# Where the modulation vectors are summed: from TensorE to VectorE, tile by tile

## Chip, cores, metric

One core of one Trainium2 chip. The metric is the device time of one execution in microseconds (us), as the median of several runs. The profile shows one execution, with the time of every instruction and DMA.

## What is computed

A backbone of two layers over 512 latent tokens and 256 context tokens, model width 1024. Every sub-layer (feed-forward half step, mixer, feed-forward half step) is wrapped in an RMSNorm with nine modulation vectors per layer: shift, scale and gate of each of the three sub-layers. There is one set for the latent tokens (from `c`) and one for the context tokens (from `c_ctx`):

```
adaln_in(x, g, m, i)     = rmsnorm(x, g) * (1 + m[3i+1]) + m[3i]
adaln_out(x, y, g, m, i) = x + w * m[3i+2] * rmsnorm(y, g)
m = silu(c) @ w_mod + b_mod          # w_mod of a layer: 1024 x (9 * 1024)
```

All is float32. The context stream ends in the mixer of layer 0 (it is read there and not written), so of the nine context vectors of layer 0 only shift, scale and gate of the first sub-layer and shift and scale of the second are used; of layer 1 none is.

## The kernel before

**Blocks.** The large products are tiled in weight blocks of 128 output columns. A block of 1024 (down stages: 768 or 640) columns per partition comes in over SP's DMA queue into `raw` (a ring of 4 slots), ScalarE makes its high part `w_hi` (`split_hi`, L893), VectorE its low part `w_lo` (`split_lo`, L1297), and TensorE runs three matmuls per 128x128 tile (`three`, L451 to L453). SP loads the next block into a slot when VectorE has split the last one; TensorE waits for `lo_split` before every block. Each engine runs its own program in order.

**Stages.** A feed-forward half step has four stages: gate-up of 24 blocks, down_a of 16 blocks of 768 columns, gate-up of 20, down_b of 16 blocks of 640. `stepped` (L92) runs them in steps of four blocks, mostly as a loop with the first and the last step unrolled. In a gate-up step, for each pair of blocks j, VectorE does two splits ahead, waits for the pair, multiplies (`prod`, L1391), waits for ScalarE's `act_hi` and subtracts (`act_lo`, L1396). In a down step it does two splits ahead, waits for the pair and copies or adds the result to `y` (L1434, L1436). The order of the stages is latent half step (0,0), context half step (0,0) with 256 tokens, the mixer, half steps (0,2), (1,0), the Hyena mixer, half step (1,2). In the context half step's first gate-up VectorE also writes the latent output (`x_out`: L1529, L1530, L1525).

**Modulation.** GpSimd loads `w_mod` in tiles of 128x1024 (512 KB, `load_mods`, L1933) into `mod_raw`, a ring of four; it issues a tile when `mod_used` says that the slot is free. A vector (a "group") is eight tiles. TensorE takes them in `mod_units` (L455): per tile k four matmuls in four column groups, with silu(c) of both streams as weights (32 columns, of which two are used) and the tile as the moving side. The units of a group stand between the blocks of a step, three, three, two and none; in the first step six after the first pair. VectorE copies the sums (`mod_copy`), TensorE turns them (`mod_turn`, L465) and VectorE adds the bias (`mod_finish`). Groups 0 and 1 are done at the start of the kernel, 2 to 7 in the first gate-up (`ffns[0][0]`), 8 in the first context gate-up (two batches of four units), layer 1's first five in the gate-up of 20 blocks of half step (0,2), its last four in down_a of half step (1,0). `gain_pre` and `gain_post` (L1345, L1353) make the scale columns from them.

**GpSimd's queue.** After layer 0's tiles it waits for the mixer, loads `rope`, clears `ak`, and goes on with the mixer's tables; then layer 1's tiles, and what Hyena needs. ScalarE's queue loads the small tables at the start, `rot` and `head_ones` among them.

Of the kernel before, what the change touches and what calls it, by code (L numbers as in the profile page):

```python
# [17 lines left out]
F32 = mybir.dt.float32  # L18
# [5 lines left out]
P = 128  # L24
# [26 lines left out]
SHIFT, SCALE, GATE = range(3)  # L51

# [61 lines left out]

def build(nc, io):
# [10 lines left out]
    for which, half0 in [(0, (0, 2)), (0, None)]:  # L126
        ffns.append([stage("gu", io["gate_up"][which, 0:24], 24, 1024, half0),
                     stage("dn", io["down_a"][which], 16, 768),
# [6 lines left out]
    for which, (half0, half1, down0) in [(1, (None, (1, 0), None)), (2, (None, None, (1, 5)))]:  # L135
# [15 lines left out]
    with ExitStack() as ctx:  # L151
# [7 lines left out]
        with ExitStack() as r:  # L159
# [5 lines left out]
            turns = r.enter_context(nc.sbuf_tensor("turns", [P, 512], F32))  # L165

# [22 lines left out]
        c_silu = sb("c_silu", [P, KT, 32])  # L189
# [11 lines left out]
        rot = sb("rot", [P, P])  # L201
        head_ones = sb("head_ones", [P, P])
# [23 lines left out]
        with region():  # L226
# [6 lines left out]
            mod_row = rb("mod_row", [P, 256])  # L233
            kept_rinv = rb("kept_rinv", [P, SEQ])

        with region():
# [4 lines left out]
            with region():  # L241
                rb("inner", [P, 32 * 256])
                rq = rb("rq", [P, 4, SEQ])
                av = rb("av", [P, ALL // P, P])
            with region():
# [22 lines left out]
        with region():  # L268
# [27 lines left out]
        mod_used, mod_row_ready, mod_turned, mod_ready = map(  # L296
            sem, ("mod_used", "mod_row_ready", "mod_turned", "mod_ready"))
# [8 lines left out]
        rope_landed = sem("rope_landed")  # L306
# [66 lines left out]
        LOADS = 8  # L373
# [68 lines left out]
        def _(pe):  # L442

            at = {"p": 0, "f": 0, "group": 0, "norm": 0, "h": 0}
# [10 lines left out]
            def mod_units(g, ks):  # L455

                for k in ks:
                    pe.wait_ge(mod_landed[k % RING], 16 * (2 * g + k // RING + 1))
                    for j in range(4):
                        ins = pe.matmul(psum[32 * j:32 * j + 32, MODP, 0:256], c_silu[:, k, :],  # L460
# [4 lines left out]
            def mod_turn(g):  # L465
# [3 lines left out]
                ins.then_inc(mod_turned, 1)  # L469

# [36 lines left out]
            def gate_up(s, T, beside=lambda i: None):  # L507
                b0, p0, g0 = s.first, at["p"], at["group"]
# [35 lines left out]
                if s.mods:  # L544
                    at["group"] += s.blocks // 4

            def down(s, T, tiles, beside=lambda i: None):
                b0, p0, g0, f0 = s.first, at["p"], at["group"], at["f"] - tiles
# [1574 lines left out]
```

## Time and profile before

| | us |
|---|---|
| median of 3 runs | 2734.34 (2731.32 to 2734.46) |
| the profiled execution | 2735.59 |
| its span, first to last instruction | 2733.9 |
| TensorE busy | 2504.0 (92%) |
| VectorE busy | 1209.1 (44%) |
| ScalarE busy | 876.5 (32%) |
| GpSimd busy | 111.7 (4%) |
| mean granted TensorE clock | 0.95 |

How to read the profile: a group of instructions is named by its line in the kernel, its engine and operation, and what it writes and reads; then come the count, the busy time and the mean ns of one, and the idle time of the engine before them with what ended it. PE is TensorE, PEld its weight loads, DVE VectorE, ACT ScalarE, POOL GpSimd, SP the sync engine. The chain of waits is followed back from the last instruction to whatever released each step. A float32 matmul that is not of the `three` kind appears as two instructions. Matmul ends are modelled and overlap, so pace is read from starts. Clock 1.00 is 2.4 GHz, 0.50 is 1.2 GHz.

### The profile page before, as it was taken

What the parts mean: (1) busy time and instruction counts of PE and PEld (TensorE: products, weight loads), DVE (VectorE), ACT (ScalarE), POOL (GpSimd) and SP (SyncE); (2) the same over time, 40 slices, a digit from 0 to 9 for tenths busy, and PEclk for the clock granted to TensorE, in tenths of its full rate; (3) what the DMA queues carried; (4) which work ended last, traced back from release to release, by engine and by line L of the source; (5) the groups of instructions that cost most, each with busy time, mean ns of one, the idle gap of its engine ahead of it and who ended that gap; (6) DMA issues with size and microseconds to landing.
All of it is one profiled execution on the core that took longest, in us unless ns stands there. A gap on an engine that the chain in (4) does not pass through costs nothing.

```text
span 2733.9 us, 32899 instructions
## 1 busy us (share of the span) xinstructions
PE 2504.0 (92%) x12514; PEld 1971.3 (72%) x12514; DVE 1209.1 (44%) x1765; ACT 876.5 (32%) x1283; POOL 111.7 (4%) x186
## 2 busy tenths in 40 slices
PE   5899999999899887899999989999989828899997
PEld 2477788899778434778877778778878527788886
DVE  4523233565553676543222353323355385533334
ACT  1422222444431456343222242222244302422222
POOL 1011000000000110000011000100000000000000
PEclk9999999999999899889999989999979969799999
DMA  7566322455312000132356312552212113132322
GB/s 289 196 219 226 128 96 75 151 176 183 130 62 83 31 1 1 62 108 85 100 200 224 130 58 93 193 181 94 91 55 93 70 46 107 49 102 81 108 77 77
DMA packets 91167, 309.53 MB, mean 113 GB/s; under 512 B 10960, under 2 KB 11632, under 8 KB 89776
## 3 DMA queue, kind: packets, MB, share of 16 engines
q1 hardware_dynamic: 67824, 221.75, 24.2%
q0 software_dynamic: 21936, 84.88, 8.7%
q8 instruction: 75, 1.23, 0.2%
q10 hardware_dynamic: 1296, 1.38, 0.1%
q14 instruction: 36, 0.29, 0.0%
HBM read 299.58 MB, written 8.39 MB: 113 GB/s over the span
## 4 chain that ended last, share of the span: by engine, by line
PE 81%; DVE 8%; ACT 4%; DMA 2%; issue 2%; POOLq 0%; POOL 0%; DVEq 0%; ACTq 0%
PE psum L451 24%; PE psum L452 23%; PE psum L453 23%; PE psum L582 2%; DMA mod_raw<-in_w_mod 2%; PE psum L460 2%; PE psum L873 1%; DVE spectrum L359 1%; DVE term L352 1%; PE psum L740 1%; PE psum L604 1%; DVE w_lo L1297 1%; PE psum L862 1%; DVE stats L1767 1%; ACT w_hi L893 0%
## 5 line engine op out<-in xcount | busy, mean ns | idle before, releaser
L451 PE MATMUL psum<-h_hi,w_hi 128*128 128x512 f32 (+1 forms) x2256 | 860.4, 381 | 28.4 <-DVE h_lo L1480 13.7
L452 PE MATMUL psum<-h_lo,w_hi 128*128 128x512 f32 (+1 forms) x2256 | 848.4, 376 | 0.0
L453 PE MATMUL psum<-h_hi,w_lo 128*128 128x512 f32 (+1 forms) x2256 | 847.5, 376 | 0.0
L451 PEld LDWEIGHTS psum<-h_hi,w_hi 128*128 128x128 f32 x2256 | 429.3, 190 | 128.1 <-issue 35.1
L1297 DVE TENSOR_TENSOR w_lo<-raw,w_hi 128x1024 fp32r<-128x1024 f32 (+2 forms) x442 | 470.6, 1100 | 65.3 <-ACT w_hi L893 61.4
L893 ACT ACTIVATE w_hi<-raw 128x1024 fp32r<-128x1024 f32 (+2 forms) x442 | 405.8, 951 | 251.2 <-PE psum L453 243.7
L453 PEld LDWEIGHTS psum<-h_hi,w_lo 128*128 128x128 f32 x2256 | 429.1, 190 | 77.2
L452 PEld LDWEIGHTS psum<-h_lo,w_hi 128*128 128x128 f32 x2256 | 429.8, 191 | 74.0 <-issue 1.0
L451 PE MATMUL psum<-act_hi,w_hi 128*128 128x512 f32 (+1 forms) x880 | 331.5, 377 | 7.5 <-DVE w_lo L1297 5.5
L453 PE MATMUL psum<-act_hi,w_lo 128*128 128x512 f32 (+1 forms) x880 | 329.2, 374 | 0.0
L452 PE MATMUL psum<-act_lo,w_hi 128*128 128x512 f32 (+1 forms) x880 | 329.1, 374 | 0.0
L1391 DVE TENSOR_TENSOR prod<-psum,square 128x512 f32<-128x512 f32 (+1 forms) x110 | 70.2, 638 | 565.5 <-PE psum L453 560.0
L923 ACT ACTIVATE act_hi<-prod 128x512 f32 (+3 forms) x110 | 64.8, 589 | 550.4 <-DVE prod L1391 550.4
L451 PEld LDWEIGHTS psum<-act_hi,w_hi 128*128 128x128 f32 x880 | 166.9, 190 | 44.5 <-issue 13.1
L453 PEld LDWEIGHTS psum<-act_hi,w_lo 128*128 128x128 f32 x880 | 166.8, 190 | 32.0
L452 PEld LDWEIGHTS psum<-act_lo,w_hi 128*128 128x128 f32 x880 | 167.0, 190 | 31.2
L921 ACT ACTIVATE square<-psum 128x512 f32<-128x512 f32 (+1 forms) x110 | 60.7, 552 | 245.2 <-PE psum L453 245.1
L1938 POOL DMA_DIRECT2D mod_raw<-in_w_mod x144 | 76.4, 530 | 1235.0 <-PE psum L460 1095.8
L1434 DVE COPY y<-psum 128x512 f32<-128x512 f32 (+3 forms) x40 | 25.5, 638 | 195.7 <-PE psum L453 195.6
L1396 DVE TENSOR_TENSOR act_lo<-prod,act_hi 128x512 f32 (+3 forms) x110 | 70.3, 639 | 91.7 <-ACT act_hi L923 91.7
L460 PE MATMUL psum<-mod_raw,c_silu 128*32 128x256 f32 x1152 | 82.3, 409 | 27.3 <-DMA mod_raw<-in_w_mod 25.1
L460 PEld LDWEIGHTS psum<-mod_raw,c_silu 128*32 128x32 f32 x1152 | 31.2, 113 | 73.1 <-DMA mod_raw<-in_w_mod 39.6
(229 smaller groups left out, 1812.5 us busy)
## 6 DMA issues: line engine op xcount, KB each, us to landing
raw<-in_gate_up SPq DMA_DIRECT2D x220, 512.0 KB, 4.2
mod_raw<-in_w_mod POOLq DMA_DIRECT2D x144, 512.0 KB, 5.6
raw<-in_down_a SPq DMA_DIRECT2D x80, 384.0 KB, 3.5
raw<-in_down_b SPq DMA_DIRECT2D x80, 320.0 KB, 3.0
raw<-in_hy_in SPq DMA_DIRECT2D x24, 512.0 KB, 3.5
raw<-in_mix_in SPq DMA_DIRECT2D x22, 512.0 KB, 3.5
filt_dram<-made SPq DMA_DIRECT2D x6, 1024.0 KB, 3.8
filt<-filt_dram POOLq DMA_DIRECT2D x2, 3072.0 KB, 10.9
```

Of the source, the lines that this page charges most:

```text
L451: pe.matmul(out, w_hi[:, slot, c:c + P], hi, start=start, stop=False)
L452: pe.matmul(out, w_hi[:, slot, c:c + P], lo, start=False, stop=False)
L453: return pe.matmul(out, w_lo[:, slot, c:c + P], hi, start=False, stop=stop)
L460: ins = pe.matmul(psum[32 * j:32 * j + 32, MODP, 0:256], c_silu[:, k, :], mod_raw[:, k % RING, 256 * j:256 * j + 256], start=(k == 0), sto ...
L582: ins = pe.matmul(psum[:, bank, t:t + 1], src[:, t * P:t * P + P], ones[:, 0:1], start=first and t == 0, stop=last and t == T // P - 1)
L893: act.activation(w_hi[:, slot, 0:cols], raw[:, slot, 0:cols], ACT.Copy).then_inc(hi_split, 1)
L921: act.activation(silu[:, j, 0:T], psum[:, bank, 0:T], ACT.Silu).then_inc(silu_ready, 1)
L923: act.activation(act_hi[:, bass.ds(2 * i + j, 1), 0:T], prod[:, j:j + 1, 0:T], ACT.Copy).then_inc(act_hi_ready, 1)
L1297: ins = dve.tensor_tensor(w_lo[:, slot, 0:cols], raw[:, slot, 0:cols], w_hi[:, slot, 0:cols].bitcast(F32), ALU.subtract)
L1391: ins = dve.tensor_tensor(prod[:, j, 0:T], psum[:, bank, 0:T], silu[:, j, 0:T], ALU.mult)
L1396: dve.tensor_tensor(act_lo[:, fl, 0:T], prod[:, j:j + 1, 0:T], act_hi[:, fl, 0:T].bitcast(F32), ALU.subtract).then_inc(act_ready, 1)
L1938: pool.dma_start(mod_raw[:, k % RING, :], io["w_mod"][layer, v, k]).then_inc(mod_landed[k % RING], 16)
```

## The change

- Groups from 2 on are summed by VectorE. `mod_add` multiplies tile k by its column of silu(c) (one value per partition) and adds it to `mod_acc` (128x1024): `tensor_scalar` for k = 0, `scalar_tensor_tensor` for the rest, each waiting for its tile and for the one before. It stands behind `act_lo` (or behind the copy to `y`), four tiles for each pair of blocks.
- TensorE only adds up over the partitions: `mod_sum`, eight matmuls of a 128x128 piece of `mod_acc` as weights against one column of ones, after the second block of the next step. VectorE adds the bias to the eight columns (`mod_keep`).
- Latent and context streams are now groups of their own. The context gets five vectors: two from groups 0 and 1, as before for both streams, and three (v = 2, 3, 4) in groups 8 to 10. That makes 21 groups instead of 18 (168 tiles instead of 144). Groups 8 to 11 (the fourth is the latent gate of sub-layer 2) are in down_a of the first half step; the context gate-up has none. Layer 1 keeps its places.
- `gain_pre` and `gain_post` wait for fixed counts and make the context's columns only where they are used.
- `mod_acc` needs room: `mod_row` and `kept_rinv` become parts of it, the context's `kept_ctx` is apart, and `rot` and `head_ones` live in the mixer's memory, loaded by GpSimd ahead of `rope` and not by ScalarE at the start. `silu(c)` is made twice, wide for groups 0 and 1 (`c_wide`) and narrow (`c_silu`).

```diff
-    for which, half0 in [(0, (0, 2)), (0, None)]:
+    for which, half0, down0 in [(0, Mods(2, 0, 2, 6), Mods(8, 0, 2, 4, 1, {3: (8, 0)})), (0, None, None)]:
...
-    for which, (half0, half1, down0) in [(1, (None, (1, 0), None)), (2, (None, None, (1, 5)))]:
+    for which, (half0, half1, down0) in [(1, (None, Mods(12, 1, 0, 5), None)), (2, (None, None, Mods(17, 1, 5, 4)))]:
...
+            def mod_sum(g):
+                pe.wait_ge(mod_used, RING + KT * g + KT)
+                for c in range(KT):
+                    ins = pe.matmul(psum[:, MODP, c:c + 1], mod_acc[:, c * P:c * P + P], ones[:, 0:1],
+                                    start=(c == 0), stop=(c == KT - 1))
+                ins.then_inc(mod_summed, 1)
+            def sum_before(s, i):
+                nonlocal pending
+                if not isinstance(i, int) or i:
+                    if s.mods:
+                        mod_sum(s.mods.first + i - 1)
+                elif pending:
+                    mod_sum(pending.first + pending.steps - 1)
+                    pending = None
...
             def gate_up(s, T, beside=lambda i: None):
...
-                        if s.mods:
-                            mod_units(g0, range(6))
+                        sum_before(s, i)
...
+                        if j == 1:
+                            sum_before(s, i)
                         if j == 2:
                             beside(i)
-                        if s.mods:
-                            mod_units(g0 + i, ((0, 1, 2), (3, 4, 5), (6, 7), ())[j])
-                    if s.mods:
-                        mod_turn(g0 + i)
...
             def first_ffns():
...
-                    elif i in (1, 2):
-                        mod_units(g, range(4 * i - 4, 4 * i))
-                    elif i == 4:
-                        mod_turn(g)
...
+            def mod_add(g, who, ks):
+                for k in ks:
+                    dve.wait_ge(mod_landed[k % RING], 16 * (2 * g + k // RING + 1))
+                    src, c = mod_raw[:, k % RING, :], c_silu[:, k, who:who + 1]
+                    if k == 0:
+                        if not isinstance(g, int) or g > 2:
+                            dve.wait_ge(mod_summed, g - 2)
+                        ins = dve.tensor_scalar(mod_acc[:, :], src, c, None, ALU.mult)
+                    else:
+                        dve.wait_ge(mod_used, RING + KT * g + k)
+                        ins = dve.scalar_tensor_tensor(mod_acc[:, :], src, c, mod_acc[:, :], ALU.mult, ALU.add)
+                    ins.then_inc(mod_used, 1)
+            def mod_keep(mods, i):
+                v, who = mods.at(i)
+                dve.wait_ge(mod_summed, mods.first + i - 1)
+                dve.tensor_tensor(mod[:, mods.layer, bass.ds(v, 1), who, :], psum[:, MODP:MODP + 1, 0:KT],
+                                  b_mod[:, mods.layer, bass.ds(v, 1), :], ALU.add).then_inc(mod_ready, 1)
+            def mods_of(s, i, j):
+                if j:
+                    keep_before(s, i)
+                if s.mods:
+                    mod_add(s.mods.first + i, s.mods.at(i)[1], range(4 * j, 4 * j + 4))
...
-                        if s.mods and j == 1:
-                            mod_copy(g0 + i)
...
                         dve.tensor_tensor(act_lo[:, fl, 0:T], prod[:, j:j + 1, 0:T], act_hi[:, fl, 0:T].bitcast(F32),
                                           ALU.subtract).then_inc(act_ready, 1)
+                        mods_of(s, i, j)
                         beside(i, j)
-                    if s.mods:
-                        mod_finish(g0 + i, s.mods[0], s.mods[1] + i)
...
-            load_mods(0)
+            load_mods(0, 0, 0, 8)
+            load_mods(8, 0, 2, 5)
+            load_mod(11, 0, 8)
             pool.wait_ge(block_done, RING + mix_in.first)
+            pool.wait_ge(mod_used, RING + 12 * KT)
+            pool.dma_start(rot[:], io["rot"]).then_inc(rot_landed, 16)
+            pool.dma_start(head_ones[:], io["head_ones"]).then_inc(rot_landed, 16)
             pool.dma_start(rope[:], io["rope"][:, 2:4]).then_inc(rope_landed, 16)
```

`down` is changed like `gate_up` on both engines. `sum_before` and `keep_before` act on the step before; the sum of a stage's last group falls into the next stage.

## Rows read from the trace of the kernel before

**Rows 1.** The page, chain that ended last: shares by engine and by line.

```profile
PE 81%; DVE 8%; ACT 4%; DMA 2%; issue 2%; POOLq 0%; POOL 0%; DVEq 0%; ACTq 0%
PE psum L451 24%; PE psum L452 23%; PE psum L453 23%; PE psum L582 2%; DMA mod_raw<-in_w_mod 2%; PE psum L460 2%; PE psum L873 1%; DVE spectrum L359 1%; DVE term L352 1%; PE psum L740 1%; PE psum L604 1%; DVE w_lo L1297 1%; PE psum L862 1%; DVE stats L1767 1%; ACT w_hi L893 0%
```

**Rows 2.** Windows, PE PEld DVE ACT POOL busy (x), clock, DMA share, GB/s.

```profile
113.67:282.24 168.57, 163.81 (x973) 120.17 (x973) 49.26 (x67) 40.64 (x52) 25.33 (x48) 0.97 0.68 238
...
349.50:458.48 108.98, 108.98 (x482) 90.28 (x481) 35.80 (x39) 29.18 (x38) 0.00 (x0) 1.00 0.27 86
...
1306.30:1373.49 67.19, 67.19 (x289) 54.08 (x288) 20.71 (x25) 15.46 (x18) 0.00 (x0) 1.00 0.32 106
1373.49:1513.19 139.70, 135.05 (x811) 98.81 (x810) 38.41 (x52) 29.16 (x38) 21.11 (x40) 0.99 0.62 217
1729.89:1819.27 89.38, 86.56 (x554) 60.45 (x552) 22.95 (x35) 15.41 (x18) 14.78 (x28) 1.00 0.69 244
```

**Rows 3.** Timeline, PE, first gate-up step: start, us, what, [idle before <- releaser].

```profile
126.15 1.93 PE L460 MATMUL psum<-mod_raw,c_silu 128*32 128x256 f32 x32
131.98 1.08 PE L460 MATMUL psum<-mod_raw,c_silu 128*32 128x256 f32 x8 [3.89 <-DMA mod_raw<-in_w_mod]
...
134.54 0.80 PE L451 MATMUL psum<-h_hi,w_hi 128*128 128x512 f32 x1
...
141.45 0.64 PE L460 MATMUL psum<-mod_raw,c_silu 128*32 128x256 f32 x8
```

**Rows 4.** Timeline, PE, second gate-up step: three units, next block.

```profile
153.85 1.50 PE L460 MATMUL psum<-mod_raw,c_silu 128*32 128x256 f32 x24
155.28 0.50 PE L451 MATMUL psum<-h_hi,w_hi 128*128 128x512 f32 x1
```

**Rows 5.** Windows of three other stretches, columns as in rows 2.

```profile
127.40:141.00 13.60, 9.24 (x55) 5.80 (x44) 3.05 (x3) 2.16 (x3) 3.17 (x6) 0.75 0.87 337
...
75.00:85.00 10.00, 10.00 (x42) 5.84 (x41) 3.92 (x11) 1.78 (x4) 0.00 (x0) 1.00 0.25 105
7.50:31.70 24.20, 9.45 (x62) 2.14 (x66) 10.87 (x21) 5.98 (x12) 3.80 (x7) 1.00 1.02 419
```

**Rows 6.** Timeline, DVE, context gate-up: pairs of splits; units stand in the first.

```profile
540.57 2.36 DVE L1297 TENSOR_TENSOR w_lo<-raw,w_hi 128x1024 fp32r<-128x1024 f32 x2 [1.31 <-ACT w_hi L893]
...
547.75 2.36 DVE L1297 TENSOR_TENSOR w_lo<-raw,w_hi 128x1024 fp32r<-128x1024 f32 x2 [1.05 <-ACT w_hi L893]
...
554.38 2.36 DVE L1297 TENSOR_TENSOR w_lo<-raw,w_hi 128x1024 fp32r<-128x1024 f32 x2 [1.04 <-ACT w_hi L893]
```

**Rows 7.** Timeline, PE: sixteen one-column matmuls and the matmul behind them.

```profile
75.63 0.95 PE L582 MATMUL psum<-ones,sumsq 128*128 128x1 f32 x8
...
77.33 0.68 PE L503 MATMUL psum<-taps,dft_f 128*128 128x512 f32 x1
```

**Rows 8.** Groups of DVE by form: busy us, mean ns, idle before.

```profile
L1297 DVE TENSOR_TENSOR w_lo<-raw,w_hi 128x1024 fp32r<-128x1024 f32 x282 | 335.4, 1221 | 45.0 <-ACT w_hi L893 41.9 <-DVE prod L1724 0.2
L1297 DVE TENSOR_TENSOR w_lo<-raw,w_hi 128x768 fp32r<-128x768 f32 x80 | 72.8, 951 | 1.0 <-ACT w_hi L893 0.3 <-DVE kept_rinv L1574 0.2
...
L1496 DVE SCALAR_TENSOR_TENSOR x<-full,gain_out,x 128x512 f32<-128x512 f32 x30 | 21.9, 742 | 0.0
```

**Rows 9.** Timeline, DVE: a tensor_scalar; the end of a gate-up step.

```profile
8.04 0.43 DVE L1373 TENSOR_SCALAR turns<-hid_arg_t 128x512 f32<-128x512 f32 x1
...
1513.31 0.69 DVE L1391 TENSOR_TENSOR prod<-psum,square 128x512 f32<-128x512 f32 x1 [5.31 <-PE psum L453]
...
1514.70 0.69 DVE L1396 TENSOR_TENSOR act_lo<-prod,act_hi 128x512 fp32r<-128x512 f32 x1 [0.70 <-ACT act_hi L923]
```

**Rows 10.** Tile mod_raw, 100 to 2000 us: landing after issue.

```profile
DMA to landing us min/median/max: 3.6/5.4/9.0
```

**Rows 11.** Timeline: GpSimd's load for the mixer, and TensorE's first rotation.

```profile
728.82 0.53 POOL L1942 DMA_DIRECT2D rope<-in_rope  x1 [186.71 <-PE psum L453]
...
750.47 1.02 PE L693 MATMUL psum<-full,rot 128*128 128x512 f32 x2
```

More of the change, by code:

```diff
@@ L112, in __init__, with at @@
         self.unrolled = False
+class Mods:
+    def __init__(self, first, layer, v, steps, who=0, other=None):
+        self.first, self.layer, self.v, self.steps, self.who, self.other = first, layer, v, steps, who, other or {}
+    def at(self, i):
+        if isinstance(i, int) and i in self.other:
+            v, who = self.other[i]
+            return v, who
+        return self.v + i, self.who
 def build(nc, io):
@@ L125, in build @@
     ffns = []
-    for which, half0 in [(0, (0, 2)), (0, None)]:
+    for which, half0, down0 in [(0, Mods(2, 0, 2, 6), Mods(8, 0, 2, 4, 1, {3: (8, 0)})), (0, None, None)]:
         ffns.append([stage("gu", io["gate_up"][which, 0:24], 24, 1024, half0),
-                     stage("dn", io["down_a"][which], 16, 768),
+                     stage("dn", io["down_a"][which], 16, 768, down0),
                      stage("gu", io["gate_up"][which, 24:44], 20, 1024),
@@ L244, in build @@
                 av = rb("av", [P, ALL // P, P])
+                rot = rb("rot", [P, P])
+                head_ones = rb("head_ones", [P, P])
             with region():
@@ L507, in gate_up @@
             def gate_up(s, T, beside=lambda i: None):
-                b0, p0, g0 = s.first, at["p"], at["group"]
+                nonlocal pending
+                b0, p0 = s.first, at["p"]
                 h0 = at["h"]
@@ L543, in gate_up @@
                 at["f"] += s.blocks // 2
-                if s.mods:
-                    at["group"] += s.blocks // 4
+                pending = s.mods
             def down(s, T, tiles, beside=lambda i: None):
-                b0, p0, g0, f0 = s.first, at["p"], at["group"], at["f"] - tiles
+                nonlocal pending
+                b0, p0, f0 = s.first, at["p"], at["f"] - tiles
                 per = tiles // 2
@@ L689, in after @@
                     if tile in ROTATED:
+                        if not rotated:
+                            pe.wait_ge(rot_landed, 32)
                         pe.wait_ge(z_copied, rotated + 1)
@@ L1032, in ffn @@
                 at["xr"] += KT
-            for dst, src in ((ident, "ident"), (b_mod, "b_mod"), (g_pre, "g_pre"), (g_post, "g_post"), (rot, "rot"),
-                             (head_ones, "head_ones"), (sink, "sink"), (ret, "ret")):
+            for dst, src in ((ident, "ident"), (b_mod, "b_mod"), (g_pre, "g_pre"), (g_post, "g_post"), (sink, "sink"), (ret, "ret")):
                 act.dma_start(dst[:], io[src]).then_inc(loaded, 16)
@@ L1345, in gain_pre @@
             def gain_pre(layer, i):
-                dve.wait_ge(mod_ready, at["group"])
-                for who in range(2):
+                dve.wait_ge(mod_ready, MODS_FOR[layer, i, SCALE])
+                for who in range(2 if (layer, i) < (0, 2) else 1):
                     ins = dve.scalar_tensor_tensor(gain_in[:, layer, i, who, :], mod[:, layer, 3 * i + SCALE, who, :], 1.0,
@@ L1353, in gain_post @@
             def gain_post(layer, i, w):
-                dve.wait_ge(mod_ready, at["group"])
-                for who in range(2):
+                dve.wait_ge(mod_ready, MODS_FOR[layer, i, GATE])
+                for who in range(2 if (layer, i) < (0, 1) else 1):
                     ins = dve.scalar_tensor_tensor(gain_out[:, layer, i, who, :], mod[:, layer, 3 * i + GATE, who, :], w,
@@ L1403, in gate_up @@
                 at["f"] += s.blocks // 2
-                if s.mods:
-                    at["group"] += s.blocks // 4
+                pending = s.mods
             def add_square(n, T, d):
```

99 lines of the change are left out of this document (51 added, 48 removed).

## The prediction

> **What bounds the kernel now.** I read the chain of waits first, then the stages by windows, then single steps. The chain says that TensorE carries 81% of the time that sets the end, nearly all of it in the three matmul lines L451 to L453; the modulation work is on it twice, as L460 (2%) and as the transfer of `mod_raw` (2%) [rows 1]. So a matmul taken from TensorE inside a feed-forward stage shortens the kernel, as long as VectorE, ScalarE and the transfers stay hidden.
>
> The windows price the modulation stage by stage. Twenty plain gate-up blocks take 108.98 us (5.449 a block), sixteen plain down blocks 67.19 us (4.20 a block) [rows 2]. With modulation in them:
> - First gate-up (24 blocks, 6 vectors): 168.57 us. Without it I take 12.48 for the first pair (113.67 to 126.15, slow because h is still being made) [rows 3] and 22 x 5.449 = 119.88, in all 132.36. The modulation costs **36.2**.
> - Layer 1 gate-up (20 blocks, 5 vectors): 139.70 - 108.98 = **30.7**.
> - Layer 1 down (16 blocks, 4 vectors): 89.38 - 67.19 = **22.2**.
>
> Two things are in that: the units themselves, three of which push the next block back by 1.43 us [rows 4], and tiles that land late. In the first step TensorE stands 3.89 us for a tile, and the block behind it takes 6.91 us (134.54 to 141.45) instead of 5.45, at a mean granted clock of 0.75 over that stretch [rows 3, 5]. A wait of TensorE for a tile is what the change can remove best: VectorE waits for it instead.
>
> VectorE is busy 49.3 of 168.6 us, 38.4 of 139.7 and 23.0 of 89.4 in the three stages [rows 2], so it has room. Whether the room lies in the right place is the question.
>
> **Removed from TensorE.** All units, turns and tile waits of the groups after the first two: 36.2 + 30.7 + 22.2 = 89.1 us. The ninth vector leaves the context gate-up, where two batches of four units stand, but that stage is paced by VectorE and ScalarE: its splits start 6.63 us apart in a half step without units and 7.18 in one with them [rows 6]. Only 2 x 0.55 = 1.1 us comes back of the 3.9 us of units. Sum **-90.2**. Bounds here: 0 and -3.9 for the context stage.
>
> **Added to TensorE.** 19 `mod_sum`, each 8 one-column matmuls over 128x128 weights, 16 instructions. The nearest row is exact in form: 16 such instructions (L582) push the next matmul from 75.63 to 77.33, 1.70 us [rows 7]. 19 x 1.70 = **+32.3**. The Trainium skill (TensorE: Matmul & The Clock Gate, "Back-to-back issue gap") gives about 81 ns a pair of weight load and matmul at 128 columns; an estimate by it is 16 x 0.081 = 1.3 us a sum, +24.6 in all. No row here is that fast (1.70 / 16 is 106 ns), and I keep the row. As bounds I take 1.4 and 2.0 us a sum, +26.6 to +38.
>
> **Added to VectorE.** Per vector one `tensor_scalar` and seven `scalar_tensor_tensor` over 128x1024. No such instruction is in the trace. At 512 columns the three-operand form takes 0.742 us; a two-operand one takes 1.221 at 1024 against 0.69 at 512, so 0.53 more for the other 512 columns: 0.742 + 0.53 = 1.27, with the wait for its own predecessor 1.29 [rows 8, 9]. The `tensor_scalar` took 0.43 at 512 [rows 9], I take 0.70. So 4.6 us in the first half of a step and 5.2 in the second, 9.8 us a vector. Bounds: 1.22 (the two-operand form) and 1.50 (twice the 512 row).
>
> **Is it covered?** A half step is two blocks. Behind the adds on VectorE stand the next two weight splits `w_lo`, and TensorE waits for those.
> - Gate-up, from the end of a pair of blocks: product to `act_lo` 2.1 (1513.31 to 1515.39), keep 0.15, adds 5.2, first split 1.2: 8.7 us, and TensorE wants it after 10.9. Slack 2.2 [rows 2, 8, 9].
> - Down: copy 0.75, keep 0.15, adds 5.2, split 0.95: 7.1 against 8.4, slack 1.3. All VectorE work of that half is 7.9 of 8.4 [rows 2, 8]. In the other half it waits about 1.1 us for `mod_sum` to release `mod_acc`, but TensorE is 1.7 later too. Nothing shows, but this is the tightest place; at 1.50 an add the first split comes at 8.0, still in time, and the second half runs 8.8 against 8.4, paid back in the other half.
> - From the layer 1 gate-up into `down_b` (0.88 of the work of a `down_a` block, about 3.5 us): adds of the last half end at 7.5, the pair of blocks at 7.0, so TensorE waits **+0.5** in `mod_sum`.
> - `mod_sum` needs the adds of the step before: done 7.5 us (down 6.1) after its last block, asked for after 10.9 (8.4).
>
> **Tiles.** The loads are still issued by POOL as tiles are used, now one every 1.3 us and not in bursts behind TensorE. They land 3.6 / 5.4 / 9.0 us after issue (min, median, max) [rows 10]; VectorE wants a tile again at least 7 us after it released it, mostly 9. A down step must move 8 x 0.52 + 4 x 0.39 = 5.8 MB in 18.5 us, 313 GB/s, against 337 in the stretch after 127.4 and 419 at the start [rows 5]. I cost it at nothing; it is covered by that slack. Three context vectors more are 24 tiles, 12.6 MB, all inside the first down stage, which moved little before. POOL's queue ends its first set there, long before its next item.
>
> **Small ones.** `rot` and `head_ones` leave ScalarE's start queue (128 KB before `ctx`; 0 to -1 us, taken as 0) and stand on POOL ahead of `rope`: 1.1 us later than 728.82 [rows 11]. The first reader is at 750.47, more than 15 us after: nothing. The second silu and the thinner `gain` steps: nothing.
>
> **Sum:** -90.2 + 32.3 + 0.5 = -57.4. The profiled execution took 2735.6 us (span 2733.9), the median of the runs shown is 1.3 lower; 2735.6 - 57.4 - 1.3 = **2677 us**. A run of this kernel tells about 0.2% (5 us) from no change.
>
> **Rivals.**
> 1. *The down stages are held by VectorE or by tiles* (0.11). The adds or a late tile overrun the 1.3 us of slack; 16 half steps, 1 us each: +16, 2693 us. For it: TensorE itself waits for tiles now [rows 3], and four more vectors come into a stage of that length. Against: the landings [rows 10]. The Trainium skill (SBUF — State Buffer, "Who interferes with whom") has a rule for it: `tensor_scalar` in its two-port mode holds the port by which GpSimd writes descriptors. The 0.43 us against 0.69 [rows 9] looks like that mode; it is 1 of 8 instructions of 0.7 us here, and would delay an issue by that much at most, which the slack takes.
> 2. *The sums bring the clock down* (0.07). Sixteen one-column matmuls are little activity. If each is followed by a stretch at 1.2 GHz as after the first wait [rows 3], where a block lost 1.5 us: 19 x 1.5 = +28, 2705 us. Against: the window with 16 of them between full matmuls has a granted clock of 1.00 (2.4 GHz) [rows 5, 7]. The Trainium skill (TensorE: Matmul & The Clock Gate, "HAM oscillation — how this bites in real kernels") lets gaps of TensorE bring the clock down again and again; by the trace gaps did and such sums did not.
> 3. *Slower: an add costs twice* (0.03). VectorE takes 8 adds of X and about 9.2 us of other work in a gate-up step of 23.5 us, 5.3 in a down step of 18.5. TensorE is held from X about 1.8 and 1.6; over 11 and 8 steps the loss is 152 X - 262 us. It eats the gain at X = 2.1. At X = 2.5 the loss is 118: 2795 us. Place: `w_lo` in every half step with adds. For it: no row has this form at 1024 columns. Against: 0.742 at 512 would have to triple.
> 4. *No change* (0.01): only if several of these met at -57.
>
> The forecast keeps 0.78. **Range:** below, sums at 1.4 us (-5.7), the whole 3.9 of the context stage (-2.8), the start (-1) and an earlier tile or two: 2664; above, rival 1 in full, rival 2 nearly, or sums at 2.0 us: 2706. Faster 0.96, same 0.01, slower 0.03.
>
> **What the profile after would show.** Right: the first gate-up stage at about 141 us, the layer 1 gate-up at 115.5, the layer 1 down at 72.3, the first down stage at 74 instead of 67.3; no L460 after 70 us; 19 groups of 16 one-column matmuls, each pushing a block by 1.7; adds of 1.27 us; VectorE waiting for `mod_raw` only here and there; granted clock 1.00 in these stages. Wrong: idle time of TensorE before L451 released by `w_lo` in the down stages (rival 1), adds above 1.6 us (rival 3), 0.9 or less in the clock column of the modulated stages (rival 2), or VectorE idle behind `mod_raw` for more than 2 us a half step.

## The result and the profile after

The changed kernel takes **2674.9 us** (median of 4 runs, 2672.8 to 2678.1) against 2734.4 before (4 runs); ratio 0.9784, 95% interval 0.9772 to 0.9795. The forecast was 2677, with a range of 2664 to 2706. The profiled execution took 2676.7, its span 2675.0.

The page of the kernel after: the total, the engines, and the chain that ended last, the counterpart of [rows 1].

```profile
span 2675.0 us, 31727 instructions
PE 2452.9 (92%) x11762; PEld 1972.4 (74%) x11762; DVE 1381.5 (52%) x1879; ACT 876.8 (33%) x1284; POOL 125.9 (5%) x212
...
PE 79%; DVE 9%; ACT 4%; DMA 2%; issue 2%; DVEq 0%; ACTq 0%; POOLq 0%; POOL 0%
PE psum L471 23%; PE psum L473 23%; PE psum L472 23%; PE psum L615 2%; DMA mod_raw<-in_w_mod 2%; PE psum L901 1%; DVE spectrum L378 1%; DVE term L371 1%; PE psum L495 1%; DVE w_lo L1326 1%; PE psum L768 1%; DVE mod_acc L1361 1%; PE psum L637 1%; ACT w_hi L921 1%; PE psum L890 1%
...
L1361 DVE SCALAR_TENSOR_TENSOR mod_acc<-mod_raw,c_silu,mod_acc 128x1024 f32<-128x1024 f32 x133 | 170.7, 1284 | 18.1 <-DMA mod_raw<-in_w_mod 11.3
```

TensorE lost 51 us of busy time and VectorE gained 172, and yet the span fell by 59: VectorE's new work lies beside TensorE's. The units (2% of the chain) are gone, the sums (L495) carry 1%. Seven stages hold the change. Windows of the kernel after, columns as in [rows 2]; they are, in order, the first gate-up, the first down_a, the 20-block gate-up, and in layer 1 the gate-up, down_b, down_a of the second half step and the gate-up behind it:

```profile
112.66:253.91 141.25, 141.25 (x656) 118.37 (x657) 97.66 (x99) 40.67 (x52) 23.31 (x44) 0.99 0.76 266
253.91:330.37 76.46, 74.51 (x354) 60.99 (x352) 59.42 (x62) 16.50 (x19) 16.95 (x32) 1.00 0.85 301
330.37:442.66 112.29, 112.29 (x496) 93.09 (x497) 40.71 (x45) 28.12 (x37) 0.00 (x0) 0.98 0.30 96
1349.77:1465.76 115.99, 115.99 (x545) 97.26 (x544) 78.07 (x78) 29.19 (x38) 19.08 (x36) 1.00 0.70 240
1465.76:1552.32 86.56, 77.11 (x353) 65.13 (x352) 43.93 (x66) 25.72 (x41) 2.12 (x4) 0.87 0.31 104
1684.96:1757.53 72.57, 72.57 (x338) 59.32 (x337) 54.38 (x55) 15.44 (x18) 14.84 (x28) 1.00 0.81 278
1757.53:1868.16 110.63, 110.63 (x497) 91.90 (x496) 41.00 (x45) 29.18 (x38) 0.00 (x0) 1.00 0.31 99
```

| stage | before | forecast | after | after, second profile |
|---|---|---|---|---|
| first gate-up | 168.57 | 141 | 141.25 | 141.43 |
| first down_a | 67.27 | 74 | 76.46 | 74.35 |
| 20-block gate-up | 108.82 | 110.5 | 112.29 | 110.61 |
| layer 1 gate-up | 139.70 | 115.5 | 115.99 | 115.99 |
| layer 1 down_b | 83.98 | 86.2 | 86.56 | 86.55 |
| layer 1 down_a | 89.38 | 72.3 | 72.57 | 72.56 |
| gate-up behind it | 108.90 | 110.6 | 110.63 | 110.64 |
| sum | 766.6 | 710.1 | 715.8 | 712.1 |

(The second profile is that of the last experiment. The prediction names the forecasts of the first, second, fourth and sixth stage; the other three are its terms added to the time before, 1.70 for the sum that falls into each and 0.5 more in down_b.) In five of the seven windows TensorE is busy for the whole time: it does not wait for VectorE there. Two places stand out. One is 1.95 us of idle time at the end of the first down stage, here in TensorE's waits in that stage (engine, line, releaser: us in total, times, longest):

```profile
PE psum L471 <- DVE w_lo L1326: 1.9, 1, 1.9
```

and the first of VectorE's waits in it:

```profile
DVE mod_acc L1361 <- DMA mod_raw<-in_w_mod: 10.2, 7, 3.0
```

VectorE waited 10.2 us for tiles in this stage, out of 11.3 in the whole run, and the splits for the next stage stood behind those waits. (In the second profile it waited 4.8 us in this stage, and TensorE not at all.) A stretch of 3.4 us at a granted clock of 0.5 followed that idle time, 331.1 to 334.5. The other is the price of a sum. Timeline of TensorE, kernel after (start, duration):

```profile
280.67 0.39 PE L473 MATMUL psum<-act_hi,w_lo 128*128 128x512 f32 x1
280.90 1.84 PE L495 MATMUL psum<-ones,mod_acc 128*128 128x1 f32 x16
282.60 0.48 PE L471 MATMUL psum<-act_hi,w_hi 128*128 128x512 f32 x1
```

The next matmul starts 1.70 us after the sum does, exactly the row of [rows 7]; it is itself slower, and from step to step a sum costs 1.76 us in a gate-up stage (23.55 against 4 x 5.449) and 1.79 in a down one (18.59 against 16.80).

### The profile page after: what moved, and what is told of

It reads as the page before. It is cut to its first block, busy times and chain, and to the rows that moved or that the text cites. A ratio compares the mean times of both kernels' runs of the same rounds, so it can differ in the third digit from the quotient of the medians.

```text
span 2675.0 us, 31727 instructions
## 1 busy us (share of the span) xinstructions
PE 2452.9 (92%) x11762; PEld 1972.4 (74%) x11762; DVE 1381.5 (52%) x1879; ACT 876.8 (33%) x1284; POOL 125.9 (5%) x212
## 4 chain that ended last, share of the span: by engine, by line
PE 79%; DVE 9%; ACT 4%; DMA 2%; issue 2%; DVEq 0%; ACTq 0%; POOLq 0%; POOL 0%
PE psum L471 23%; PE psum L473 23%; PE psum L472 23%; PE psum L615 2%; DMA mod_raw<-in_w_mod 2%; PE psum L901 1%; DVE spectrum L378 1%; DVE term L371 1%; PE psum L495 1%; DVE w_lo L1326 1%; PE psum L768 1%; DVE mod_acc L1361 1%; PE psum L637 1%; ACT w_hi L921 1%; PE psum L890 1%
## 5 line engine op out<-in xcount | busy, mean ns | idle before, releaser
L473 PEld LDWEIGHTS psum<-act_hi,w_lo 128*128 128x128 f32 x880 | 166.5, 189 | 32.3
L1361 DVE SCALAR_TENSOR_TENSOR mod_acc<-mod_raw,c_silu,mod_acc 128x1024 f32<-128x1024 f32 x133 | 170.7, 1284 | 18.1 <-DMA mod_raw<-in_w_mod 11.3
L1993 POOL DMA_DIRECT2D mod_raw<-in_w_mod x168 | 89.3, 531 | 977.6 <-DVE mod_acc L1358 583.1
L901 PE MATMUL psum<-idft,spectrum 128*128 128x256 f32 x128 | 33.2, 428 | 56.0 <-DVE spectrum L378 56.0
```

The source lines that it names most:

```text
L473: return pe.matmul(out, w_lo[:, slot, c:c + P], hi, start=False, stop=stop)
L901: ins = pe.matmul(psum[:, 4 + n % 2, i * HB:i * HB + HB], y_f[c][:, i, m, t * P:t * P + P], idft[:, m, :], start=(m == 0), stop=(m == 3))
L1361: ins = dve.scalar_tensor_tensor(mod_acc[:, :], src, c, mod_acc[:, :], ALU.mult, ALU.add)
L1993: pool.dma_start(mod_raw[:, k % RING, :], io["w_mod"][layer, v, k]).then_inc(mod_landed[k % RING], 16)
```

## Experiments

**A sum made twice.**

```diff
-                for c in range(KT):
+                for c in list(range(KT)) + list(range(KT)):
                     ins = pe.matmul(psum[:, MODP, c:c + 1], mod_acc[:, c * P:c * P + P], ones[:, 0:1],
```

> The changed kernel with the eight one-column matmuls of `mod_sum` issued twice (the second pass computes the same sums again). Theory: the sums lie on TensorE's path at their full price, for VectorE, ScalarE and the transfers have slack in every modulated stage. After: a sum pushes the next block by 1.7 to 1.8 us, so 19 more cost +32 to +34, about 2708 us, the granted clock of the stages unchanged. Rival, the sums bring the clock down: twice the stretch of one-column matmuls should then show a granted clock under 1.00 behind the sums and cost more than +34, up to +60 if half of them are followed by a block at half clock. Rival, the sums partly lie in time that TensorE would wait for `w_lo` anyway: less than +25.

Measured: 2744.6 us (6 runs, 2739.0 to 2749.7), ratio 1.0038 (1.0024 to 1.0051). That is 70 us over the changed kernel and 10 over the kernel before: the whole gain is gone. Windows of this kernel for TensorE (PE busy, clock, DMA share, GB/s): one double sum, the 3.4 us just behind it, and the stretch after that.

```profile
226.49:230.00 3.51, 3.51 (x34) 1.00 0.85 328
230.60:234.00 3.40, 3.40 (x10) 0.50 0.49 176
234.20:237.40 3.20, 3.20 (x16) 1.00 0.87 282
```

TensorE did not stop (32 starts from 226.49 to 229.86, 0.11 apart; busy 3.51 of 3.51), but with 32 one-column matmul instructions in a row (two for each float32 matmul) the clock fell to 1.2 GHz for 3.4 us. Such a stretch goes with 17 of the 19 double sums; it begins between 1.9 us before the last of the 32 starts and 1.4 us behind it. Six times it lasts 6.8 us: 78 us at half clock in all, which costs 39. With 19 x 1.79 = 34 for the work that makes 73; the same seven stages took 783.2 us here against 712.1 in the second profile, 71 more. So the first rival of this run holds, and goes past the +60 that it gave as its upper end; the theory covers only half of the loss.

**The same work, apart.** A second set of eight one-column matmuls at the end of the step, two blocks behind the sum.

```diff
+            def idle_sum():
+                for c in range(KT):
+                    pe.matmul(psum[:, MODT, c:c + 1], ident[:, :], ones[:, 0:1], start=(c == 0), stop=(c == KT - 1))
...
+                    if summed:
+                        idle_sum()
```

> The changed kernel with a second set of eight one-column matmuls behind every sum, but two blocks later and not right behind it (weights `ident`, into a PSUM bank that these stages do not use; result not used). As many instructions more on TensorE as in the run with the sums issued twice, which lost 70 us where 33 were expected, with a granted clock of 0.5 for 3.4 or 6.8 us behind 17 of its 19 double sums. Theory: it is the length of the unbroken stretch of one-column matmuls that brings the clock down (32 in a row), not their number; 16 in a row leave it at 1.00, wherever they stand: +19 x 1.76 = +33, 2708 us, no half clock in the modulated stages. Rival, it is their share of a longer time: half clock behind many of them again, +50 to +70.

Measured: 2704.4 us (4 runs), ratio 0.9887 (0.9872 to 0.9902), 28 over the changed kernel on the same chip. Windows of the first gate-up and the first down stage:

```profile
112.22:262.64 150.42, 150.42 (x736) 0.99 0.72 252
262.64:344.12 81.48, 81.48 (x418) 1.00 0.82 286
```

Against the second profile these are nine microseconds more for five sets and 7.1 for four. From 117 to 515 us and in the modulated stages of layer 1 the granted clock never fell. There are as many one-column matmuls as in the run before, and the time is 40 us less: the length of the unbroken run decides, not their number. (The second set has another matrix as weights, `ident`; that the weights' content plays a part is not excluded by this run alone. The next one has `mod_acc` throughout.)

**A sum and a half.** The first four columns made twice: 24 instructions in a row.

```diff
-                for c in range(KT):
+                for n, c in enumerate(list(range(4)) + list(range(KT))):
                     ins = pe.matmul(psum[:, MODP, c:c + 1], mod_acc[:, c * P:c * P + P], ones[:, 0:1],
-                                    start=(c == 0), stop=(c == KT - 1))
+                                    start=(c == 0), stop=(n in (3, 11)))
```

> The changed kernel with twelve one-column matmuls in a sum (24 instructions of the profile, 2.6 us) instead of eight: the first four are made twice, with the same result. It asks how far the kernel is from the point at which the clock falls. Work alone: 19 x 0.88 = +17, 2692 us. If the point lies beyond 24 instructions, that is all and the clock stays at 1.00 in the modulated stages; if below, half clock behind most sums, 1.7 to 3.4 us each: +50 or more, 2725 us or over. I give the first 0.5, the second 0.3, something between (behind some of the sums) 0.2.

Measured: 2710.0 us (4 runs), ratio 0.9906 (0.9891 to 0.9922), 33 over the changed kernel on the same chip. Two stretches behind sums, same columns: the sum at 198.04 was followed by half clock, the one at 224.13 by full clock.

```profile
201.80:205.00 3.20, 3.20 (x9) 0.50 0.88 303
227.00:236.00 9.00, 9.00 (x41) 1.00 0.86 299
```

The clock fell behind 12 of 19 sums, for 48 us in all, which costs 24. It was the third case, the one I gave 0.2. What separates the 7 from the 12 the runs don't show.

**One more add's worth on VectorE**, in each half step behind the four adds:

```diff
                 if s.mods:
                     mod_add(s.mods.first + i, s.mods.at(i)[1], range(4 * j, 4 * j + 4))
+                    src = x[:, 0:2, :].rearrange("p a b -> p (a b)")
+                    dve.scalar_tensor_tensor(full[:, :, :].rearrange("p a b -> p (a b)"), src, c_silu[:, 0, 0:1], src,
+                                             ALU.mult, ALU.add)
```

> The changed kernel with one more `scalar_tensor_tensor` over 128x1024 (1.28 us, operands in SBUF, result not used) behind the four adds of each half step, 38 in all. Theory (the slack of the prediction: 2.2 us in a gate-up half step, 1.3 in a down one): nothing in the gate-up stages (0 to +1), 0 to +0.3 a half step in the 16 modulated down half steps; together 0 to +5, 2675 to 2680 us. Rival, the down stages are already held by VectorE: +1.28 in each of the 16 down half steps, +20, 2695 us. Rival, VectorE is on the path in every modulated half step: +1.28 x 38 = +49, 2724 us.

Measured: 2676.7 us (4 runs), ratio 0.9784 (0.9767 to 0.98), the ratio of the changed kernel itself. 38 x 1.28 = 49 us of VectorE work cost nothing that the times can tell; in the trace the first down stage, down_b and the layer 1 down_a are 0.4, 1.8 and 0.4 us longer than in the second profile of the changed kernel. The sum of 2.6 is what the theory allowed, but most of it stands where the theory did not look: in down_b TensorE waits 0.7 us for a split behind the pending sum.

**And 0.75 us on top of it.** As above, and behind it:

```diff
+                    dve.scalar_tensor_tensor(psum[:, MODT, :], x[:, 2, :], c_silu[:, 0, 0:1], x[:, 2, :],
+                                             ALU.mult, ALU.add)
```

> As the run with one more, and a second extra instruction of 512 columns behind it (about 0.75 us), so 2.03 us more VectorE work a half step. Theory: in a down step VectorE then has 5.3 + 9.8 + 4.1 = 19.2 us of work against 18.5 of TensorE, so it becomes the bound there: +0.7 to +1.5 a step over 8 steps, +6 to +12; in a gate-up step 9.2 + 9.8 + 4.1 = 23.1 against 23.5, still hidden on the mean, though the half step with the longer chain (8.7 + 2.0 = 10.7 against 10.9) is at its edge: 0 to +3. Together +6 to +15, 2681 to 2690 us, with idle time of TensorE in front of L451 released by `w_lo` in the down stages. Rival, VectorE already holds the down stages: +2.03 x 16 = +32, 2707 us. Rival, there is more slack than was worked out: 0.

Measured: 2681.8 us (4 runs), ratio 0.981 (0.9794 to 0.9826), 7 us over the changed kernel by the medians, at the low end of what was expected. The intervals of the two ratios just touch (0.9794 and 0.9795), so the traces have to say more. Windows of two down steps of layer 1 in this kernel (columns as in [rows 2]):

```profile
1711.43:1729.67 18.24, 18.24 (x87) 14.97 (x86) 18.03 (x20) 3.39 (x4) 4.24 (x8) 1.00 0.91 314
1729.67:1748.17 18.50, 18.50 (x89) 15.17 (x89) 18.13 (x21) 3.81 (x4) 4.24 (x8) 1.00 0.96 320
```

and all of TensorE's waits from the start of that stage to just behind its end:

```profile
PE psum L471 <- DVE w_lo L1326: 1.2, 1, 1.2
```

VectorE is busy 18.03 of 18.24 us, not 19.2 as I had counted, and TensorE still does not wait inside this stage, only 1.2 us at its end. The slack is just used up here. Against the second profile of the changed kernel the first down stage is 2.1 us longer, down_b 3.1 and the layer 1 down_a 1.6. In the first down stage TensorE waits 0.40 and 0.30 us inside and 0.9 at the end. In down_b it waits for a split right behind the sum, and then the clock falls (timeline of TensorE; then windows of it: sum and wait, the stretch behind, the one after that):

```profile
1469.69 1.95 PE L495 MATMUL psum<-ones,mod_acc 128*128 128x1 f32 x16 [0.66 <-DVE mod_acc L1361]
1473.09 0.47 PE L471 MATMUL psum<-act_hi,w_hi 128*128 128x512 f32 x1 [1.45 <-DVE w_lo L1326]
...
1469.69:1473.09 3.40, 1.95 (x16) 1.00 0.79 292
1474.00:1477.20 3.20, 3.20 (x9) 0.50 0.72 242
1477.60:1481.00 3.40, 3.40 (x16) 1.00 0.60 191
```

So 3.1 us are 1.45 of idle time and 1.7 for 3.4 us at half clock. In the changed kernel the longer half step of such a step looks like this (timeline of VectorE): copy, keep, four adds of 1.31, split.

```profile
1720.67 0.69 DVE L1497 COPY y<-psum 128x512 f32 x1 [2.18 <-PE psum L473]
1721.28 0.16 DVE L1368 TENSOR_TENSOR mod<-psum,b_mod 128x8 f32 x1
1721.35 5.24 DVE L1361 SCALAR_TENSOR_TENSOR mod_acc<-mod_raw,c_silu,mod_acc 128x1024 f32<-128x1024 f32 x4
1726.51 0.95 DVE L1326 TENSOR_TENSOR w_lo<-raw,w_hi 128x768 fp32r<-128x768 f32 x1
```

The 2.18 us in front of it, and 0.73 and 0.87 us in front of the copy and the `tensor_scalar` of the other half, are the slack: 3.8 us a step. The two extra instructions overlap with their neighbours and take 1.85 us of VectorE's time and not 2.03 (starts at 1726.08 and 1727.93 in this run), 3.7 a step. They fill it.

**Smaller tiles in the first down stage**, in the changed kernel:

```diff
-            load_mods(8, 0, 2, 5)
-            load_mod(11, 0, 8)
+            load_mods(8, 0, 2, 5, 128)
+            load_mod(11, 0, 8, 128)
```

> The changed kernel with only 128 of the 1024 columns loaded for each tile of groups 8 to 11 (those of the first down stage); the adds and sums are as they were, on stale columns, so these modulation vectors are wrong. It takes 11.0 MB out of 76 us. Two theories for what the first down stage and the block behind it cost over the prediction (76.5 us against 74; TensorE idle 1.95 us at its end and then some blocks at half clock): (a) late transfers, of gate-up weights and of `mod_raw`, which share the queues with these 32 tiles: the idle time and the half clock go, VectorE no longer waits for `mod_raw`, -2 to -5 us, 2670 to 2673. (b) VectorE's own work: the idle time stays, 2675.

Measured: 2673.4 us (4 runs), ratio 0.9775 (0.9759 to 0.9792), not to be told from the changed kernel. In the trace the stage took 74.35 us and the next 110.61, 3.8 less than in the first profile after. VectorE's waits in the stage, first line:

```profile
DVE y L1497 <- PE psum L473: 9.4, 7, 2.2
```

On VectorE nothing waits for `mod_raw` any more. That fits (a), but the last run below takes most of its weight away. (The edit takes 32 x 0.46 = 14.7 MB out, not 11.0.)

**Smaller tiles in the kernel before.** The same edit there, from the third group of layer 0 and the second of layer 1 on.

> The kernel before with only 128 of the 1024 columns loaded for each tile of the modulation groups from the third of layer 0 and from the second of layer 1 on; units, turns and waits are unchanged, so most modulation vectors are computed from stale columns. It separates the two things in the 89 us that the prediction took off as one term: TensorE's own work for units and turns, and its waits for tiles. Theory: a batch of three units pushes a block by 1.43 us, 0.48 a unit; 120 units and 15 turns of 0.3 in the three stages are 62 us, so the rest, 27 us, is waits for tiles and the half clock that follows them. With tiles of an eighth these should be gone but for a small rest: -15 to -27, 2707 to 2719 us. Rival, the units themselves cost nearly all of it (they are longer in a batch of four with a turn): 0 to -5, 2729 to 2734 us.

Measured: 2723.5 us (7 runs), ratio 0.9969 (0.9958 to 0.998), so -8.5 us: outside both expectations, nearer the rival. The three modulated stages of [rows 2] came down by 3.2, 0.7 and 3.7 us, 7.5 in all. TensorE's waits for tiles in the layer 1 gate-up stage were 4.7 us before and still 3.0 here:

```profile
PE psum L460 <- DMA mod_raw<-in_w_mod: 3.0, 1, 3.0
```

That one is the stage's first tile; in the first gate-up 2.4 us of such waits stayed. Half clock stayed too, behind both (windows of TensorE, this kernel):

```profile
130.60:133.80 3.20, 3.20 (x17) 0.50 0.94 298
1379.90:1386.50 6.60, 6.21 (x26) 0.50 0.95 384
```

These two stretches last 3.4 and 6.8 us, as long together as the two of the kernel before, and cost 5.1. So of the 89 us some 71 (less 7.5 that went, 5.4 of waits and 5.1 of half clock that stayed) were TensorE's own work. The steps say the same. In this kernel the first units of two steps start 26.63 us apart in the gate-up (1402.41 and 1429.04) and 21.44 in the down stage (1724.17 and 1745.61), against 21.80 and 16.80 without units: 4.83 and 4.64 us a vector, 72 us for the fifteen. My price of 62 us was low, in part because of what stands at both ends of a batch (timeline of TensorE, this kernel):

```profile
1409.21 0.39 PE L453 MATMUL psum<-h_hi,w_lo 128*128 128x512 f32 x1
1409.53 1.50 PE L460 MATMUL psum<-mod_raw,c_silu 128*32 128x256 f32 x24
1410.96 0.50 PE L451 MATMUL psum<-h_hi,w_hi 128*128 128x512 f32 x1
1411.29 0.39 PE L452 MATMUL psum<-h_lo,w_hi 128*128 128x512 f32 x1
```

Starts stand 0.32 apart going in and 0.33 behind the first matmul coming out, where matmuls in a row are 0.23 apart. From 1409.21 to 1411.29 are 2.08 us instead of 0.45: 1.63 for three units, 1.43 of it between the marks of [rows 4]. The Trainium skill (TensorEngine Tiling (Array Packing), "Key Properties") says that changing the tiling mode drains TensorE; these rows agree, with about 0.2 us for going there and back; that it is a drain they don't show.

**Groups 8 to 11 one stage later**, in the 20-block gate-up:

```diff
-    for which, half0, down0 in [(0, Mods(2, 0, 2, 6), Mods(8, 0, 2, 4, 1, {3: (8, 0)})), (0, None, None)]:
+    for which, half0, half1 in [(0, Mods(2, 0, 2, 6), Mods(8, 0, 2, 4, 1, {3: (8, 0)})), (0, None, None)]:
...
-                     stage("dn", io["down_a"][which], 16, 768, down0),
-                     stage("gu", io["gate_up"][which, 24:44], 20, 1024),
+                     stage("dn", io["down_a"][which], 16, 768),
+                     stage("gu", io["gate_up"][which, 24:44], 20, 1024, half1),
```

> The changed kernel with groups 8 to 11 moved from the first down stage (16 blocks of 4.2 us) to the gate-up stage of 20 blocks behind it, where half steps are longer (10.9 us against 8.4) and less has to be moved per us; that stage is unrolled for it. Theory: the sums cost the same there, the idle time of 1.95 us at the start of that stage and the 1.7 us of half clock behind it go: -3 to -4, 2671 us. Rival, late transfers come back at the next boundary or the unrolled stage costs code loading: 0 or up to +3.

Measured: 2677.1 us (5 runs), ratio 0.9805 (0.9791 to 0.9818): no gain. The two stages took 69.0 + 116.0 = 185.0 us, 3.7 less than in the first profile of the changed kernel, as expected, but not less than in its second (74.35 + 110.61).

**Packed sums.** A matrix of ones as weights, `mod_acc` as moving data on four column groups; copy and turn behind it.

```diff
-                for c in range(KT):
-                    ins = pe.matmul(psum[:, MODP, c:c + 1], mod_acc[:, c * P:c * P + P], ones[:, 0:1],
-                                    start=(c == 0), stop=(c == KT - 1))
+                for j in range(4):
+                    ins = pe.matmul(psum[32 * j:32 * j + 32, MODP, 0:256], ones[:, 0:32], mod_acc[:, 256 * j:256 * j + 256],
+                                    start=True, stop=True, tile_position=(0, 32 * j))
...
+                    dve.wait_ge(mod_summed, g - 1)
+                    dve.tensor_copy(full[:, 1, 0:256], psum[:, MODP, 0:256]).then_inc(mod_row_ready, 1)
```

> The changed kernel with the sum over the partitions made the other way round: a 128x32 matrix of ones as weights and `mod_acc` as the moving data, four matmuls of 256 columns on four column groups of TensorE, as the old units did, then a copy to SBUF by VectorE (0.3 us) and two transposes (as the old turn), at the end of the next step. 4 short matmuls and 2 transposes in place of 16 instructions with 128x128 weights. Theory: what a sum costs is its instructions with full weights (0.11 us each), so about 0.45 for a batch like one unit of the old kernel and 0.3 for the turn, 0.75 against 1.79 us: -1.04 x 19 = -20, 2655 us. Rival, the turn at the end of the step makes TensorE wait for VectorE's copy, or the four matmuls do not run side by side: a sum at 1.5 or more, -5 to +5.

Measured: 2664.1 us (5 runs), ratio 0.9749 (0.9736 to 0.9762): faster than the changed kernel by some 10 us, half of what was expected. A vector costs 1.05 us from step to step (22.85 against 21.80), not 0.75. The four matmuls take 0.57, with the same 0.1 us more in the starts of the neighbours on either side (timeline of TensorE, this kernel); the rest is the turn.

```profile
1395.18 0.39 PE L473 MATMUL psum<-h_hi,w_lo 128*128 128x512 f32 x1
1395.50 0.64 PE L495 MATMUL psum<-mod_acc,ones 128*32 128x256 f32 x8
1396.07 0.50 PE L471 MATMUL psum<-h_hi,w_hi 128*128 128x512 f32 x1
1396.41 0.39 PE L472 MATMUL psum<-h_lo,w_hi 128*128 128x512 f32 x1
```

The turn at the last step of a down stage waits for the copy, which stands behind two splits on VectorE (timeline of TensorE):

```profile
1743.44 0.44 PE L488 MATMUL psum<-ident,full 128*128 128x128 f32 x2 [1.27 <-DVE full L1388]
```

**Both edits.**

> Both of the last two edits together: packed sums, and groups 8 to 11 in the 20-block gate-up stage. If they are independent, the gains add: -20 - 3.7, 2651 us. If the idle time at the first down stage's end was set by the sums' place, less than the sum.

Measured: 2661.7 us (5 runs), ratio 0.974 (0.9726 to 0.9754), 10 us short of the expectation, nearly all of it from the packed sum (9 us short by itself).

**The changed kernel and the last version, side by side.**

> The changed kernel once more, unaltered, for a second profile and times on the same chip as the version with both edits. Theory: the 1.95 us of idle time at the end of the first down stage is a matter of when transfers land in one execution (two other runs that add work to VectorE there showed 0.2 and 0.9), so it is 0 to 2 us again and the stage 74.4 to 76.5; the other modulated stages are the same within 0.3 us; 2672 to 2678 us.

> Packed sums and groups 8 to 11 in the 20-block gate-up stage, once more, beside the changed kernel on the same chip. From the first time: 13 us faster than the changed kernel (2661.7 against 2674.9), ratio to before 0.974.

Measured: 2676.5 us (5 runs; ratio 0.9787, 0.9773 to 0.9801) and **2662.6 us** (5 runs; 0.9733, 0.9719 to 0.9747). The version with both edits is 14 us faster, the intervals are apart. Nearly all of it is the packed sum; that moving the groups adds anything is not shown. Windows of the second profile of the changed kernel, first down stage and the next:

```profile
253.53:327.88 74.35, 74.35 (x353) 61.15 (x352) 59.47 (x61) 15.44 (x18) 16.89 (x32) 1.00 0.88 311
327.88:438.49 110.61, 110.61 (x497) 91.88 (x496) 41.00 (x45) 29.19 (x38) 0.00 (x0) 1.00 0.30 98
```

and of the version with both edits, the first two stages and the third, PE alone:

```profile
114.88:252.63 137.75, 137.75 (x627) 0.99 0.78 270
252.63:320.89 68.26, 68.26 (x301) 1.00 0.43 146
320.89:433.90 113.01, 113.01 (x521) 1.00 0.61 213
```

The changed kernel, profiled a second time, has no idle time and no half clock at that boundary: the 1.95 us of the first profile belong to the landings of one execution. They are no fixed cost, and smaller tiles or another stage had little to win.

## Why the prediction was right, point by point

- **Removed, 90.2.** The three stages came out within 0.5 us of 141, 115.5 and 72.3. It was safe to price the old work by whole stages; priced by units and turns I would have had 62 us, as the expectation of the smaller tiles in the kernel before shows. Its opening claim, that a wait of TensorE for a tile is what the change removes best, was overweighted: smaller tiles alone brought 7.5 us of 89, and TensorE's own work, some 71, was the bulk.
- **The context stage, 1.1.** Right: that gate-up stage and the stage behind it took 113.49 us before and 112.41 after, 1.08 less.
- **Added to TensorE, 32.3.** The sum of 1.70 from [rows 7] counts to the start of the next matmul; 1.76 to 1.79 from step to step are 1.4 us more over 19. By row it was 4% low. At 110 ns an instruction it is farther still from the 81 ns of the Trainium skill (TensorE: Matmul & The Clock Gate, "Back-to-back issue gap").
- **Added to VectorE.** 1.284 us for a lone add and 1.31 in a row (forecast 1.27 and 1.29), 0.750 for the `tensor_scalar` (0.70). GpSimd's issues of tiles took 0.53 us at the median and 0.67 at most, so the port rule that rival 1 cites does not show in their length. The down half step came out as worked out: 0.69 + 0.16 + 5.24 + 1.8 = 7.9 us.
- **Slack of 2.2 and 1.3 us.** Safe, and for the down stages too small: 1.28 us more a half step cost nothing that the times tell, and the 1.85 us of the two extra instructions, more than 1.3, still left TensorE without a wait inside the layer 1 down stage. A whole down step has 3.8 us of room, where the forecast's count gives 18.5 - 15.1 = 3.4. The 2.2 of the gate-up is confirmed from below only (1.85 fits); no run went beyond it. Where the slack ends is at the stage ends and behind the pending sum in down_b.
- **+0.5 into down_b.** TensorE waited 0.66 us before that sum, and the stage is 2.6 longer where 2.2 were forecast.
- **Tiles at nothing.** Right on the mean and not safe in each execution: 3.8 us in the first profile (1.95 idle, the rest at half clock), 0 in the second.
- **Rival 1** didn't come: 0 to 2 us of waits in the first down stage, none in the layer 1 down_a. **Rival 3** neither: an add is far from 2.1. **Rival 2** was refused for a good reason, since [rows 5, 7] show one set of sixteen at full clock; 19 of 19 such sums stayed at 1.00 here too. But its price if it came was understated and its nearness not seen. I took 1.5 us behind each sum; at half again the length half clock stood behind 12 of 19, at 2.0 us each (24 / 12), at double length behind 17 of 19, at 2.3 us each (39 / 17), and double sums took the whole gain.
- **The total.** Some of the accuracy is luck. In the seven stages the first profile gained 50.8 us and not 56.5; everything else gained 8.1 and not about 1. Against the second profile it is 54.5 and 4.5. Of the rest, the start gave 1.0 and 1.6 and the context stage 1.1. Most of what is left lies between the first block of the mixer of layer 0 and the first down stage behind it, where the change moves only two small loads: 575.3 us before, and 568.5 and 572.4 in the two profiles after, at a mean granted clock of 0.93, 0.94 and 0.93. The kernel before with smaller tiles, whose mixer code is the old one, took 568.6 at 0.94; of the ten profiles of variants of the changed kernel six show 568.4 to 568.6 and two 572.2 and 572.4. So this part differs by up to 7 us from one profile to the next with the clock's pattern, and the runs show no effect of the change in it.
- **Slips in the forecast's own working.** None moved the total. The layer 1 gate-up is 115.8 by its terms (108.98 + 4 x 1.70), not 115.5; measured 115.99. A down_b block has 0.83 of the work of a down_a block (3.50 against 4.20 us), not 0.88; the 3.5 us that the term of 0.5 goes by are right. With adds of 1.50 us the first split would come at 7.9, not 8.0.

## What to carry to other kernels

Price what leaves the bounding engine by the whole stage that it leaves, and what joins another engine by the slack of one half step there, with the order of that engine's queue written out; then fill that slack on purpose to see where it ends, and look at the ends of the stages first. Before a reduction over partitions is put on TensorE as a run of thin matmuls, look at the clock behind it and not only at its length: keep such runs short and apart. Where one execution shows a stall of a microsecond or two behind a transfer, take a second profile before you move work for it.

## What the runs showed of the hardware that I had not expected

- The granted clock fell with TensorE busy throughout. Behind 24 one-column matmul instructions in a row it fell 12 times of 19, behind 32 17 of 19, to 1.2 GHz for 3.4 or 6.8 us each. Behind 16 it stayed at 1.00, 19 times of 19 in both profiles of the changed kernel, and in the run with the same work apart 38 of 38. The one exception among the variants with single sums is the one shown above, where TensorE stood idle for 0.66 us before the 16 and 1.45 behind them. The Trainium skill (TensorE: Matmul & The Clock Gate, "HAM oscillation — how this bites in real kernels") explains such drops by gaps in which TensorE waits; here there was none at the runs of 24 and 32, but for 0.66 us in front of the one in down_b.
- Going from full-width matmuls to four column groups and back costs about 0.2 us in the starts of the neighbours, so packed work pays in batches and less in single calls.
